# Smaller row transfers for x and the output, later small transposes, and earlier loads of layer two's preparation in a two-layer macaron kernel

## What is computed

```python
for l in range(DEPTH):
    x = x + 0.5 * swiglu(rmsnorm(x, norm_ffn1[l]), ffn1_w_in[l], ffn1_w_out[l])
    z = rmsnorm(x, norm_mix[l]) @ mix_w_in[l]
    u_ssm, u_gm, v_gm = z[..., :512], z[..., 512:1024], z[..., 1024:]
    y_ssm = s5_group(u_ssm, ...)        # diagonal complex state space, 32 groups of 16 channels
    y_gm = gmlp_group(u_gm, v_gm, ...)  # causal spatial gating in chunks of 128
    y = jnp.concatenate([rmsnorm(y_ssm, ...), rmsnorm(y_gm, ...)], axis=-1)
    x = x + y @ mix_w_out[l]
    x = x + 0.5 * swiglu(rmsnorm(x, norm_ffn2[l]), ffn2_w_in[l], ffn2_w_out[l])
return rmsnorm(x, norm_final)
```

## Time and profile before

| | us |
|---|---|
| median of 3 runs | 996.09 (994.89 to 996.38) |
| the profiled execution, its time | 994.81 |
| its span, first to last instruction | 993.1 |
| TensorE busy in the span | 951.5 (96%) |
| VectorE, ScalarE, GpSimd busy | 560.8, 469.9, 399.2 |
| mean granted TensorE clock | 0.988 of full |

### The profile page before, as it was taken

The page is one execution under the profiler, slowest core; times in us unless marked ns, Lnnn a source line. Parts: engine busy times, 40 slices in busy tenths (PEclk is TensorE's granted clock), DMA queues, the critical chain, the costliest instruction groups (busy, mean ns, idle before and its releaser), DMA issues.

```text
span 993.1 us, 12019 instructions
## 1 busy us (share of the span) xinstructions
PE 951.5 (96%) x4640; PEld 797.3 (80%) x4640; DVE 560.8 (56%) x620; ACT 469.9 (47%) x670; POOL 399.2 (40%) x610
## 2 busy tenths in 40 slices
PE   3899999999999999999999999999999999999992
PEld 2688888888898888888788888888889888888882
DVE  1455665438867555664346555544687755555442
ACT  3444444347546544543345444443655554454431
POOL 3688998727620588998851000000253000000000
PEclk9899999999999999999999999999999999999997
DMA  6755555434224865555435656555532365665521
GB/s 182 205 186 192 174 172 209 170 128 170 85 85 151 232 212 172 175 194 184 150 104 186 196 178 200 174 191 191 170 127 85 127 198 184 192 199 182 206 91 42
DMA packets 128980, 165.10 MB, mean 166 GB/s; under 512 B 16916, under 2 KB 108188, under 8 KB 128924
## 3 DMA queue, kind: packets, MB, share of 16 engines
q1 hardware_dynamic: 128400, 163.51, 51.1%
q10 hardware_dynamic: 524, 0.82, 0.3%
HBM read 163.27 MB, written 1.05 MB: 165 GB/s over the span
## 4 chain that ended last, share of the span: by engine, by line
PE 74%; POOL 17%; DVE 3%; issue 2%; DMA 1%; ACT 1%; SPq 1%; DVEq 0%; POOLq 0%; ACTq 0%
PE bank L339 22%; PE bank L341 21%; PE bank L340 21%; POOL pt L1087 4%; POOL sc L1087 4%; POOL bp L1087 2%; POOL sc L1090 2%; PE bank L395 1%; PE bank L588 1%; PE bank L545 1%; PE bank L531 1%; DMA raw<-in_ffn_w_in 1%; DVE w_lo L857 1%; PE bank L468 1%; POOL cw L1093 1%
## 5 line engine op out<-in xcount | busy, mean ns | idle before, releaser
L857 DVE TENSOR_TENSOR w_lo<-raw,w_hi 128x1024 fp32r<-128x1024 f32 x304 | 391.4, 1292 | 334.9 <-ACT w_hi L650 334.6
L650 ACT ACTIVATE w_hi<-raw 128x1024 fp32r<-128x1024 f32 x304 | 321.2, 1060 | 317.5 <-PE bank L341 307.1
L339 PE MATMUL bank<-w_hi,x_hi 128*128 128x512 f32 x864 | 345.1, 399 | 1.2 <-DVE x_lo L872 1.2
L341 PE MATMUL bank<-w_hi,x_lo 128*128 128x512 f32 x864 | 339.0, 392 | 0.0
L340 PE MATMUL bank<-w_lo,x_hi 128*128 128x512 f32 x864 | 338.5, 392 | 0.0
L341 PEld LDWEIGHTS bank<-w_hi,x_lo 128*128 128x128 f32 x864 | 163.4, 189 | 35.2
L339 PEld LDWEIGHTS bank<-w_hi,x_hi 128*128 128x128 f32 x864 | 163.6, 189 | 33.5 <-issue 1.6
L340 PEld LDWEIGHTS bank<-w_lo,x_hi 128*128 128x128 f32 x864 | 163.8, 190 | 32.3
L1096 POOL TENSOR_TENSOR rstd_c<-ms_c,neg_half 128x2 f32<-128x2 f32 (+1 forms) x8 | 9.4, 1181 | 427.2 <-DVE ms_c L877 427.2
L339 PE MATMUL bank<-w_hi,h_hi 128*128 128x512 f32 x352 | 139.4, 396 | 0.0
L341 PE MATMUL bank<-w_hi,h_lo 128*128 128x512 f32 x352 | 137.7, 391 | 0.0
(11 more groups left out here) (138 smaller groups left out, 715.2 us busy)
## 6 DMA issues: line engine op xcount, KB each, us to landing
raw<-in_ffn_w_in SPq DMA_DIRECT2D x174, 512.0 KB
raw<-in_ffn_w_out SPq DMA_DIRECT2D x44, 1024.0 KB
raw<-in_mix_w_in SPq DMA_DIRECT2D x12, 1024.0 KB
raw<-in_mix_w_out SPq DMA_DIRECT2D x8, 1024.0 KB
raw<-in_ffn_w_in SPq DMA_DIRECT2D x4, 256.0 KB, 5.2
x<-in_x ACTq DMA_DIRECT2D x2, 256.0 KB
x<-in_x SPq DMA_DIRECT2D x2, 256.0 KB
ws_raw<-in_gm_w_s SPq DMA_DIRECT2D x2, 256.0 KB
```

Source lines behind the costliest of these rows:

```text
L339: mm(o, hi_a, hi_b, start=first, stop=False)
L341: return mm(o, lo_a, hi_b, start=False, stop=last)
L650: A(w_hi[:, n % RING, :], raw[:, s, (n % 2) * 1024:(n % 2) * 1024 + 1024], ACT.Copy).then_inc(hi_done, 1)
L857: TT(w_lo[:, n % RING, :], raw[:, s, (n % 2) * 1024:(n % 2) * 1024 + 1024], w_hi[:, n % RING, :].bitcast(F32), ALU.subtract).then_inc(lo_d ...
```

## The change

Four edits:

1. x is loaded in 16 transfers of 32 rows, one for each j, where there were 4 of 128 rows; the output is stored in 8 transfers of 32 rows where there were 3. SyncE stores six of them and ScalarE two; both now wait for both column halves of h = 1.
2. TensorE's small transposes stand in the middle of up block 1 for both layers. For layer one that is half a block later than before, for layer two half a block earlier. ScalarE's copy to `sv` moves with them, and layer two's `prep_c` moves one block earlier.
3. SyncE issues layer two's 22 preparation transfers after layer one's output-projection weights and ahead of ffn2's first weights, behind waits for the last state-space sum (`y_done`) and for GpSimd's last copy of the gate weights (`gw_done`). Before, they stood after up block 2's weights.
4. GpSimd runs `prep_first(1)` before ffn2's `norm` and no longer after it.

```diff
-PREP_SMALL = (0, 1)
+PREP_SMALL = (0, 0)
...
-                    if p == 1 and b == 2:
-                        sp.wait_ge(half_done, half(0, UP2))
-                        load_small(1)
-                        load_c(1)
-                        load_late(1)
...
-                sp.dma_start(x[:, 0, c * 512:c * 512 + 512], xv[0, :, :, c * 512:c * 512 + 512]).then_inc(x_full[c][0], 16)
+                w = slice(c * 512, c * 512 + 512)
+                for j in range(T):
+                    sp.dma_start(x[32 * j:32 * j + 32, 0, w], xv[0, j, :, w]).then_inc(x_full[c][0], 16)
...
+                if l + 1 < DEPTH:
+                    sp.wait_ge(y_done, l * 2 + 2)
+                    sp.wait_ge(gw_done, l + 1)
+                    load_small(l + 1)
+                    load_c(l + 1)
+                    load_late(l + 1)
                 load_ffn(l, 1)
...
             sp.wait_ge(fin_done[0], 2)
-            sp.dma_start(ov[0], x[:, 0, :]).then_inc(stored, 16)
-            sp.wait_ge(fin_done[1], 1)
-            sp.dma_start(ov[1, :, :, 0:512], x[:, 1, 0:512]).then_inc(stored, 16)
-            sp.wait_ge(stored, 3 * 16)
+            for j in range(T):
+                sp.dma_start(ov[0, j], x[32 * j:32 * j + 32, 0, :]).then_inc(stored, 16)
+            sp.wait_ge(fin_done[1], 2)
+            for j in range(2):
+                sp.dma_start(ov[1, j], x[32 * j:32 * j + 32, 1, :]).then_inc(stored, 16)
+            sp.wait_ge(stored, 2 * T * 16)
...
                     if hh == 1 and b:
                         hidden_turn(l, j, b - 1)
+                    if hh == 1 and f < DEPTH and b == PREP_SMALL[f] + 1:
+                        prep_small(f, bank[2 * ROLES[l, stage_of(2 * j)][3]])
...
                     if f < DEPTH:
-                        if b == PREP_SMALL[f]:
-                            prep_small(f, bank[2 * t1_])
...
-                        if h == 4 * PREP_SMALL[f] + 7:
+                        if f == 0 and h == 7:
+                            act.wait_ge(gain_t, 2)
+                            A(gains[:, KT * DEPTH:GAINS], bank[2 * t1_ + 1][:, KT * DEPTH:GAINS],
+                              ACT.Copy).then_inc(gain_done, 1)
+                        if h == 4 * PREP_SMALL[f] + 9:
                             prep_small(f, bank[2 * t1_])
-                            if f == 0:
-                                act.wait_ge(gain_t, 2)
-                                A(gains[:, KT * DEPTH:GAINS], bank[2 * t1_ + 1][:, KT * DEPTH:GAINS],
-                                  ACT.Copy).then_inc(gain_done, 1)
...
-                act.dma_start(x[:, 1, c * 512:c * 512 + 512], xv[1, :, :, c * 512:c * 512 + 512]).then_inc(x_full[c][1], 16)
+                w = slice(c * 512, c * 512 + 512)
+                for j in range(T):
+                    act.dma_start(x[32 * j:32 * j + 32, 1, w], xv[1, j, :, w]).then_inc(x_full[c][1], 16)
...
-            act.dma_start(ov[1, :, :, 512:1024], x[:, 1, 512:1024]).then_inc(stored, 16)
+            for j in range(2, T):
+                act.dma_start(ov[1, j], x[32 * j:32 * j + 32, 1, :]).then_inc(stored, 16)
...
+                if l + 1 < DEPTH:
+                    prep_first(l + 1)
                 norm(norm_no(l, 2))
...
             mix(0)
-            prep_first(1)
             prep_rest(1)
```

More of the change, by code:

```diff
@@ L346, in x_turn @@
                 if l == 0 and i == 0:
-                    pe.wait_ge(x_full[c][h], 16)
+                    pe.wait_ge(x_full[c][h], 16 * T)
                 else:
@@ L661, in squares @@
                 if l + i == 0:
-                    act.wait_ge(x_full[c][t], 16)
+                    act.wait_ge(x_full[c][t], 16 * T)
                 else:
```

## The result

| | before | after |
|---|---|---|
| median of four runs each, us | 996.11 (994.89 to 996.38) | 971.02 (969.25 to 973.48) |
| ratio, 95% interval | | 0.9752 (0.9729 to 0.9775) |
| profiled execution: time, span, us | 994.81, 993.1 | 970.62, 968.9 |
| TensorE busy, us | 951.5 | 948.6 |

The forecast was 970.2. The total came out nearly as forecast because errors of opposite sign met: the two ends gained more than forecast, and between them a part of the gain was given back at a place that the prediction had not worked out. The lines of after are numbered 5 to 8 higher than those of before: the long matmuls are L344 to L346, `w_hi` is L655, the groups' turn of `w1` is L471, and its copy on GpSimd L1281.

A forecast was written before the change was run, and what follows sets the result against it. TensorE was taken as the bound, busy 951.5 of 993.1 us, so only its 41.6 us without matmuls and low clock counted. Gains 8.7 + 6.2 + 7.0 + 4.0 = 25.9 off the 996.09 median gave 970.2 us, range 966.5 to 978.

The forecast's parts named there:

- The end: Final output stores: 32-row transfers use all 16 DMA engines, not 4; end 8.7 us earlier, bounds 7 to 11.4.
- The start: Loading x before the first matmul: ScalarE's issuing becomes last; first matmul at 11.9, 6.2 us earlier, bounds 3.3 to 7.
- The rival at 0.86 us a piece: Start: ScalarE pays 0.86 us for each x piece, start gains only 3.3 us, total 973.1; chance 0.13.
- The small transposes of layer one: Up block 1: TensorE's 4.17 us wait for `bs_p` and 2.87 us of low clock go, together 7.0 us.
- What is late next: Layer one's groups: GpSimd loses 6.6 us against TensorE; 1.9 us of margin left at the third group, still covered.
- Layer two's groups: Layer two's preparation: TensorE's 2.4 us of waits for `w1` and 1.54 us of low clock go, together 4.0 us.
- The moved loads: SyncE's 22 transfers ahead of ffn2: its first chunk lands by 300.9, 3.4 us of cover; cost nothing.
- The rival of too short a cover: Layer one's small transposes or groups: a 2 us pause remains with 2.9 us of low clock, total 975.1; chance 0.12.

The follow-up runs named there:

- the two variants without it: Layer one's load_c and load_late issued after up block 2's weights, on the changed kernel, run on two occasions: 967.04 us and 966.80 us.

## Why the prediction was right, point by point

- **The end: 8.7 forecast, 10.1 measured.** The mechanism (four engines of sixteen) is shown by the stores of 64 rows. The mis-sized term is the stretch from VectorE's last result to the end: I allowed 984.0 - 979.3 = 4.7 us and the 0.4 us of span behind the wait, 5.1 together; it took 968.9 - 965.2 = 3.7. I had leaned to the upper of my two bounds, to account for all of the old wait; on the prediction's scale the last wait's end came out at 979.3 + 3.7 - 0.4 = 982.6, nearer to the lower, 981.3.
- **The start: 6.2 forecast, 6.6 measured**, by the chain that was named: ScalarE's eight pieces at 0.50 us, the gains done at 8.62 (8.9 forecast), `w_hi`, `w_lo`, `x_lo`, first matmul at 11.51 (11.9). The rival at 0.86 us a piece is out.
- **The small transposes of layer one: 7.0 forecast.** The wait of 4.17 and the slow matmuls of the earlier trace rows are gone in after. But alone on the kernel before, this edit was worth 3.1 us in the one run made, and the 2.87 us of low clock in the sum is no fixed price: behind a wait of 3.91 us it was 1.6 and 1.5 us in the two kernels that changed x or the output alone.
- **What is late next: the step that failed.** I started `prep_rest(0)` at 33.8 and found 1.9 us of slack at the third group. It began at 36.20. TensorE had no wait at the third group, its piece being done at 192.83 + 1.29 = 194.1 against 197.65; but these 3.5 us of margin come from the 3.7 us of delay at the second group. That one I gave no number for. In before TensorE reached it at 196.47, with the piece done at 185.77 + 1.28 = 187.05 after a wait of 1.52. That is 10.9 us of margin, and with TensorE 13.2 earlier and GpSimd 6.6 earlier 4.3 would be left: more than at the third, and still it was late. It lost 2.4 us because `sv` came late: I had put ScalarE's wait for block 2's weights at nothing, having cost SyncE's queue at nothing up to 20 us and not looked at 26. It lost 3.7 more because GpSimd itself took longer from `b1h` to the piece, 147.6 us where it had been 143.9 (145.4 less the wait of 1.52); the prediction had this pace as unchanged, without a reason. The sentence "I am wrong if ScalarE waits for a DMA between the first matmul and block 2" named the place; it was the right thing to look for.
- **Layer two's groups: 4.0 forecast.** The waits of 2.4 us are gone. GpSimd started `prep_rest(1)` at 322.69, as forecast 6 us earlier against TensorE (338.51 before, less the 9.7 us by which TensorE reaches this part earlier, 279.66 against 269.97). The experiment that puts the transposes back by one block confirms it from the other side (4.71 us). The clock part of the term, 1.54, is not a fixed saving: two kernels with the same pause of 1.49 us paid none of it.
- **The moved loads: nothing forecast, nothing measured.** SyncE issued them in 285.07 - 271.95 = 13.1 us (13.06 forecast), and ScalarE's splits behind them still wait for TensorE, not for data:

```profile
285.07 25.61 SPq L241 DMA_DIRECT2D raw<-in_ffn_w_in  x10
```
```profile
291.83 1.06 ACT L655 ACTIVATE w_hi<-raw 128x1024 fp32r<-128x1024 f32 x1 [0.68 <-PE bank L346]
```

- **The rival of too short a cover** happened in part: a pause of 2 us with its clock came back, at a group of layer one, for 3.7 us instead of the 4.9 of its price. Without it the gain would have been 24.2 + 3.7 = 27.9 us by this estimate; the traces of the two variants without it have spans of 963.8 and 965.0, 29.3 and 28.1 below before's. That the number came out so close is luck: 1.8 us too little at the two ends stood against 3.5 too much between them. The second set of executions of the same kernel had a median of 967.01, 3 us under the forecast.

Open: why GpSimd took 147.6 us for the same instructions. Its busy time shows it (window from `b1h` to the piece, before and after; the fifth figure of busy time is GpSimd's), and its waits don't:

```profile
40.37:185.70 145.33, 145.33 (x672) 120.45 (x671) 80.52 (x80) 65.62 (x84) 126.12 (x227) 0.99 0.57 186
```
```profile
36.20:183.70 147.50, 146.90 (x683) 121.62 (x681) 82.68 (x83) 68.37 (x87) 129.73 (x226) 1.00 0.57 187
```

129.7 us against 126.1 for 226 and 227 instructions: single instructions were longer. It is not one kind alone, nor one way alone: the 16 operations `bp<-pt` of 128x256 took 1.20 us each in after and 0.92 before, 4.5 us in all, while the two `pt<-sc,cosn` of 128x128 took 0.41 us in after and 1.37 before. In the other kernels the stretch took 144.3 to 147.3 us. No run was made for the cause.

## What to carry to other kernels

Look at the outermost dimension of a transfer on the DRAM side (32 here in place of 4), above all where nothing else runs beside it: that was 17 of the 24 us here. When an engine's step is moved past others in its queue, follow the whole chain behind it (here ScalarE's `sv`, then 145 us of GpSimd, then TensorE) and put a margin to every place where it is collected, not to one. A margin under 4 us at the end of such a stretch was none here: GpSimd's time for the same work moved by 3.7 us.

## What the runs showed of the hardware that I had not expected

- **The price of a pause in clock is not fixed by its length.** After 1.49 us at layer two's group the clock fell in before (window 0.50, seven slow matmuls) and stayed in two kernels; after a pause of only 0.93 us it fell in the kernel with layer one's small transposes alone. Behind `bs_p` 4.17 us of wait left 14 slow matmuls before, 3.91 us left eight and seven. After 2.09 us at the same place in the same kernel eight matmuls took 3.41 us once, and the twelve from 187.97 to 193.24 took 5.27 the other time: 1.6 and 2.5 us lost. The Trainium skill, TensorE: Matmul & The Clock Gate, section "Part 1: The HAM clock gate", says that the number of slow matmuls at the start of one kernel varies from run to run; these rows show the same behind a pause in the middle. The kernel before ranged over 991.3 to 996.4 us; how much of that is clock was not traced.
- **The granted clock doesn't show everything.** From 11 to 14 us its column shows 1.00, and yet the first twelve matmuls are 0.43 us apart, the pace of a stretch at 0.50; with transposes ahead of them they are 0.23 apart under the same 1.00.
- **Transfers in short runs fill the DMA engines without moving much.** The window of the earlier trace rows in which weights came at 343 GB/s with a share of 1.04 holds the preparation's last loads in after:

```profile
24.00:27.00 3.00, 3.00 (x14) 2.21 (x13) 2.37 (x3) 2.69 (x5) 2.70 (x5) 1.00 0.80 132
```

A share of 0.80 for 132 GB/s: of the packets that start in this window, 2269 have 64 bytes each, and they take 0.48 of the 0.80. The weights of block 2 are issued right behind them, at 26.59, and are there at 33.48.
